# One encoder layer on one core: gating sum on VectorE inside the search rounds, and half-wide transposes for the queries

## The chip, the cores and the metric

One Trainium2 chip, of which the kernel uses one core. The metric is the time on the device of one execution, in microseconds (us). The engines are named as the profile names them: PE (TensorE, its matmuls), PEld (TensorE's weight loads), DVE (VectorE), ACT (ScalarE), POOL (GpSimd) and SP (SyncE).

## The reference, cut to what matters

One layer runs over 1024 prompt rows (tiles 0 to 7 of 128 rows) and 32 sample rows with a cache of 1024 positions (tile 8). The normalised input is projected to q, k, v, the indexer's qi, ki and wi, and u and vs. Every query scores all keys with the indexer, keeps the best 256 and attends over them. Beside it runs a gating unit. Both are concatenated and go through an output projection, a residual sum and a feed-forward block.

```
def _sgu(u, vs, ln_g, ln_b, w_s, b_s):
    u = gelu(u); vs = gelu(vs)                     # 4 groups of 128 channels
    vn = layer_norm(vs) * ln_g + ln_b
    s = einsum('gij,bcjge->bcige', wm, vn) + b_s   # over chunks of 128 positions
    return u * s

logits = einsum('bthd,btkhd->bthk', q, kg) * (HEAD_DIM ** -0.5)
```

The part of the gating unit that the change moves is `u * (W_s vn + b_s)`. Of the attention it changes how q gets from rows to columns.

## The kernel before, in words

**Precision.** Nearly every matmul splits its operands into a high and a low float16 half and runs three of the four products; weights are scaled by WS = 64.

**Order of the work.** The seven projections are made one after the other, in the order qi, ki, vs, u, k, v, q (`CHUNKS`, L61), each over the nine tiles. One tile of one projection is a step. Each engine has an instruction stream of its own, written out by hand as a `step` function, and parts of a step lag one or two tiles behind. `lagged(part, c, t, rep, lag)` calls a part for the tile `lag` before. Engines wait for each other by semaphores that count up.

**A step on PE** (L994): in u first the spatial product of the gating unit (`spatial`, L928, 12 matmuls into PSUM bank 6 or 7), then the projection (`main`, L911, 24 matmuls of 512 columns into bank 2 or 3, which waits for the evacuation of the projection two before), then the transposes of the tile two before (`post`, L940, into bank 4 or 5).

**A step on ACT** (L1471): `dup_q` for q (of the tile two before), the evacuation `E` (L1292; L1311 for u, L1316 for q and k, L1301 for v) into e32, the first sign count of the search, the cast `H` (L1319, L1346) of the tile before into the buffers hl, in u the evacuation of the spatial product `sgu_evac` (L1362, L1367: four 128x128 operations that scale and add the bias b_s, into r32), `R` (L1388, L1405), which takes the transposes of the tile two before out of PSUM, and the second sign count with the sum L1468. In the first two steps of each projection it casts weight pieces too (L438).

**A step on POOL** (L800): `A` (L716) makes the rotary embedding in four operations (L742 to L747) out of e32 into r32; for u it multiplies r32 (the gating sum) with e32 (gelu of u), L727. `B` (L749, L774) then subtracts the cast of the tile before, which gives the low half.

**The search on DVE.** From u to the fourth step of q the threshold of the best 256 keys is searched bit by bit, in 31 rounds (`bit_round`, L1864). A round counts five score tiles on DVE (L1833) and two on ACT (L1464), then waits for ACT's counts (L1839, the judge) and flips the bits (L1845). ACT's first sign count of the next round waits for that. Round b belongs to step b of u, k, v, q. In some rounds DVE also splits a weight piece (L444). After the search DVE makes the masks of the first four tiles (L1903 to L1918) and waits for the first logits (`peak`, L1941).

**Queries.** q needs each head's 64 columns turned, and the result twice, in partitions 0 to 63 and 64 to 127, once for the high half (unit 0) and once for the low half (unit 1). `H` writes every head's high half twice side by side into one buffer hl (1024 columns), `B` writes the low half into the other one, and `dup_q` (L1360) copies it beside itself. PE then turns 128 columns at a time, 8 transposes a unit. So one tile of q takes both buffers, and the cast of a tile waits until the split of the tile before has read it, and the split until PE has turned the tile before. At the end of q the last tiles are flushed (`flush`, L403): the last cast, two conversions of the cache (L1450), the last copies and evacuations. PE's first logits, DVE's first peaks and POOL's clearing of the packed queries wait for the last of them.

The loops over the steps 2 to 7 are hardware loops with two steps in a round, except where `LOOP` (L409) and the callers unroll them.

## Time and profile before

| | |
|---|---|
| median of 3 runs | 1440.9 us (1438.02 to 1442.58) |
| the profiled execution | 1443.37 us |
| its span, first to last instruction | 1441.6 us |
| granted TensorE clock, mean | 0.951 |
| busy shares | PE 90%, PEld 64%, DVE 57%, ACT 50%, POOL 35% |

The profile shows one execution. Times in it count from the start of the span. A line of a timeline has the start, the duration (of a merged run of equal instructions from the first start to the last end), engine, line of the kernel, operation, output and inputs, count, and in brackets the idle time of the engine before it with what ended it. M is the one large SBUF tensor, PS the PSUM, small a tensor of small values. The projections qi to q run until 478 us, the attention until 662 us, the output projection until 778 us, the feed-forward block to the end. The stage u runs from about 236 to 299 us, k to 356 us, v to 404 us, q to 478 us.

### The profile page before, as it was taken

The page shows a single profiled execution, that of the slowest core. Times are in us where ns is not written, and L with a number is a line of the kernel's source. Part 1 is how long each engine was busy: PE and PEld are TensorE (multiplying, and loading weights), DVE is VectorE, ACT ScalarE, POOL GpSimd, SP SyncE. Part 2 cuts the span into 40 slices and gives each one's busy share as a digit, 9 for nine tenths or more (in the row PEclk, how much of TensorE's full clock was granted, in tenths as well). Part 3 has the DMA queues.
Part 4 walks back from the last instruction along what each step waited for, and adds up shares of the span by engine and source line. Part 5 has one row for each costly group of instructions (what it writes and reads, how often), then busy time and mean ns, then how long its engine had stood idle before and what let it go on. Part 6 is the DMA issues. An engine that isn't in the chain of part 4 may idle for free.

```text
span 1441.6 us, 29366 instructions
## 1 busy us (share of the span) xinstructions
PE 1293.2 (90%) x10636; PEld 928.2 (64%) x10636; DVE 816.8 (57%) x1495; ACT 717.5 (50%) x1408; POOL 498.9 (35%) x542
## 2 busy tenths in 40 slices
PE   6868887999996666798997999999999998999997
PEld 3443333544443445565555888888888887888886
DVE  5324675889988565896656555666565552212022
ACT  5455788888784844893434444444444441001011
POOL 5872436367258531443003333333333300000001
PEclk9988999999999579999998999999999999999999
DMA  6121001212100310114231222112222127211013
GB/s 240 45 64 33 15 3 44 59 37 83 66 18 0 88 37 17 45 31 140 88 107 39 60 58 58 47 42 56 58 58 58 29 91 205 65 60 38 0 31 91
DMA packets 81597, 86.70 MB, mean 60 GB/s; under 512 B 6768, under 2 KB 63120, under 8 KB 81520
## 3 DMA queue, kind: packets, MB, share of 16 engines
q1 hardware_dynamic: 76112, 75.07, 18.1%
q10 hardware_dynamic: 4992, 9.51, 1.8%
q0 software_dynamic: 416, 1.08, 0.2%
q8 instruction: 49, 0.80, 0.2%
q14 instruction: 28, 0.23, 0.0%
HBM read 72.34 MB, written 13.31 MB: 59 GB/s over the span
## 4 chain that ended last, share of the span: by engine, by line
PE 55%; DVE 5%; ACT 4%; issue 2%; POOL 1%; DMA 1%; SPq 1%; POOLq 0%; ACTq 0%; DVEq 0%
PE PS L1189 29%; PE PS L1246 15%; PE PS L1152 6%; DVE M L1952 1%; PE PS L1069 1%; PE PS L1046 1%; DVE M L1941 1%; PE PS L1099 1%; ACT M L1542 1%; DMA M<-in_w_down 1%; ACT M L1531 1%; SPq L653 1%; PE PS L1233 1%; PE PS L1166 0%; PE PS L1066 0%
## 5 line engine op out<-in xcount | busy, mean ns | idle before, releaser
L1189 PE MATMUL PS<-M 128*128 128x264 f16 x3696 | 420.8, 278 | 9.6 <-ACT M L1646 9.6
L1189 PEld LDWEIGHTS PS<-M 128*128 128x128 f16 x3696 | 363.2, 98 | 66.6 <-ACT M L1646 10.2
L923 PE MATMUL PS<-M 128*128 128x512 f16 (+1 forms) x1512 | 309.4, 366 | 0.5 <-DVE M L1754 0.4
L1246 PE MATMUL PS<-M 128*128 128x256 f16 x2112 | 233.2, 274 | 6.6 <-DVE M L2166 6.6
L923 PEld LDWEIGHTS PS<-M 128*128 128x128 f16 (+1 forms) x1512 | 139.8, 104 | 153.1 <-issue 13.9
L1246 PEld LDWEIGHTS PS<-M 128*128 (+1 forms) x2112 | 207.2, 98 | 32.2 <-issue 7.5
L1833 DVE TENSOR_SCALAR_CACHE_REDUCE M<-M,small 128x384 f16<-128x384 f32 (+5 forms) x162 | 132.9, 881 | 0.8
L872 POOL TENSOR_TENSOR M<-M 128x264 f32<-128x264 f32 x44 | 34.7, 789 | 283.4 <-ACT M L1646 283.4
L688 POOL TENSOR_TENSOR small<-small 128x1 f32<-128x1 f32 x18 | 3.4, 189 | 317.1 <-ACT M L1738 237.3
L2005 DVE SCALAR_TENSOR_TENSOR M<-M 128x2048 f16<-128x2048 f32 (+1 forms) x44 | 88.9, 2025 | 36.1 <-ACT M L1584 36.1
L2166 DVE SCALAR_TENSOR_TENSOR M<-PS,M 128x256 f32 (+1 forms) x32 | 13.6, 424 | 165.3 <-PE PS L1246 165.3
L1646 ACT ACTIVATE M<-PS 128x264 f32<-128x264 f32 x132 | 51.3, 388 | 100.8 <-PE PS L1189 88.2
L1152 PE MATMUL PS<-M 128*128 128x512 f16 x384 | 84.2, 379 | 0.0
L1669 ACT ACTIVATE M<-M 128x1024 f16<-128x1024 f32 (+1 forms) x24 | 22.7, 978 | 117.1 <-PE PS L1233 82.7
L1464 ACT ACTIVATE M<-M,small 128x1056 f16<-128x1056 f32 x62 | 72.8, 1174 | 11.2 <-DVE small L1845 10.4
L1584 ACT ACTIVATE M<-M 128x2048 f16<-128x2048 f32 (+1 forms) x44 | 74.2, 1688 | 0.0
L1656 ACT ACTIVATE M<-M 128x264 f32 (+1 forms) x88 | 37.2, 423 | 70.2 <-DVE M L2090 36.3
L1069 PE MATMUL PS<-ident,M 128*128 128x128 f32 x306 | 57.0, 298 | 16.8 <-DVE M L1952 10.4
L1952 DVE TENSOR_TENSOR M<-PS,M 128x512 f16<-128x512 f32 (+3 forms) x102 | 53.5, 549 | 28.1 <-ACT M L1542 27.4
L2082 DVE TENSOR_TENSOR M<-PS,M 128x264 f32<-128x264 f32 x44 | 18.9, 432 | 83.7 <-PE PS L1189 82.3
L1152 PEld LDWEIGHTS PS<-M 128*128 128x128 f16 x384 | 37.5, 98 | 43.5
L1046 PE MATMUL PS<-M 128*128 128x512 f16 (+3 forms) x240 | 56.5, 361 | 9.5 <-DVE small L1941 8.1
(178 smaller groups left out, 1947.8 us busy)
## 6 DMA issues: line engine op xcount, KB each, us to landing
M<-in_w_in SPq DMA_DIRECT2D x24, 512.0 KB, 3.7
M<-in_w_gate SPq DMA_DIRECT2D x22, 512.0 KB, 4.0
M<-in_w_up SPq DMA_DIRECT2D x22, 512.0 KB, 5.2
M<-in_w_down SPq DMA_DIRECT2D x20, 512.0 KB, 4.1
M<-in_x_prompt SPq DMA_DIRECT2D x16, 512.0 KB, 5.0
M<-in_w_out SPq DMA_DIRECT2D x8, 512.0 KB, 3.8
h_scratch<-M ACTq DMA_DIRECT2D x8, 512.0 KB, 5.1
M<-h_scratch SPq DMA_DIRECT2D x16, 256.0 KB, 7.7
```

The source lines that it names most:

```text
L923: last = pe.matmul(bank(b)[:, 0:w], xnT[:, ds(t, 1), k, s, :].squeeze(1), wt[wbuf(c)][:, k * w:(k + 1) * w], start=(k == 0 and i == 0), st ...
L1046: last = pe.matmul(PSf[:, l_bank(j) * 512 + c0:l_bank(j) * 512 + c0 + n], qT[:, t, s, hd, :], key[:, hd, c0:c0 + n], start=(s == 0 and hd ...
L1069: last = pe.transpose(bank(pt_bank(g))[:, i * P:(i + 1) * P], LP[j % 4][:, (b0 + i) * P:(b0 + i + 1) * P], ident[:])
L1152: last = pe.matmul(bank(2 * p + d), mixT[:, t, k, s, :], wt[d][:, k * 512:(k + 1) * 512], start=(k == 0 and i == 0), stop=(k == KT - 1 and ...
L1189: last = pe.matmul(o, wsp[x][:, zw, wb, k * P:(k + 1) * P], ablk[:, ab, za, k * HT + s * SC:k * HT + (s + 1) * SC], start=(name not in kep ...
L1246: last = pe.matmul(o[:, 0:256], cols[:, ds(m * SC + r * P, P)], wt[dc % 2][:, f, :], start=(f == 0 and i == 0), stop=(f == FT - 1 and i == 2))
L1464: act.activation(sign_out, scores[:, o:o + TOK], ACT.Sign, scale=-1.0, bias=kth[:, j:j + 1], accum_out=signs[:, i:i + 1]).then_inc(signs_s ...
L1584: act.activation(wsp[x][:, 0, 4 * half:7 if half else 4, :], tb if half else raw[x], ACT.Copy, scale=WS).then_inc(w2_hi, 1)
L1646: act.activation(buf[s], bank(BANKS[x][s]["a"])[:, 0:SC], ACT.Copy).then_inc(kept, 1)
L1833: dve.tensor_scalar(dump[x][:, 0:S], scores[:, o:o + S], kth[:, j:j + 1], None, ALU.is_ge, ALU.add, accum_out=cnt[:, j:j + 1]).then_inc(se ...
L1952: dve.tensor_tensor(r[:, 1, 0:x * P], bank(pt_bank(g))[:, 0:x * P], r[:, 0, 0:x * P], ALU.subtract).then_inc(pt_ready, 1)
L2005: dve.scalar_tensor_tensor(out=wsp[x][:, 1, b, :], in0=tb if half else raw[x], scalar=WS, in1=wsp[x][:, 0, b, :], op0=ALU.mult, op1=ALU.su ...
```

## The change

The spatial product stays in PSUM. In round t + 1 of the search, behind its five counts and before its judge, DVE makes for each of the four groups one operation `(PSUM + bias) * gelu(u)`, in place in e32 (`gate`). The bias is scaled by 64 once, on POOL, at the first step of vs, so the gated value is 64 times as large as before. The cast and the split of u read e32; ACT's evacuation of the spatial product and POOL's multiplication are gone. So that the attention's half of the concatenated input has the same scale, its normalisation multiplies by 64, and the output projection scales by 1/64 twice.

For q the cast writes 512 columns into the first half of a buffer hl, the split writes the low half into its second half, and the next tile takes the other buffer. `dup_q` is gone. PE turns each head's 64 columns twice, into partitions 0 to 63 and 64 to 127: 16 transposes a unit in place of 8. PE's loop over the tiles of q is unrolled.

The diff, cut to its core:

```diff
@@ n_rope
-            return before(c, lambda n: n not in ("vs", "v")) + t
+            return before(c, lambda n: n not in ("vs", "u", "v")) + t
@@ wait_e_free
                 if NAMES[u[0]] == "vs":
                     eng.wait_ge(vs_norm, u[1] + 1)
+                elif NAMES[u[0]] == "u":
+                    eng.wait_ge(sub_done, n_cast(*u) + 1)
                 else:
                     eng.wait_ge(r_ready, n_rope(*u) + 1)
@@ POOL: A
                 if name == "u":
-                    pool.wait_ge(spatial_evac, t + 1)
-                    pool.wait_ge(evac_done, n_step(c, t) + 1)
-                    pool.tensor_tensor(r32[p], r32[p], e32[p], ALU.mult).then_inc(r_ready, 1)
                     return
@@ POOL: B
-                r = r32[p]
+                r = e32[p] if name == "u" else r32[p]
...
                 elif name == "q":
-                    pool.wait_ge(post_done, n_unit(c, t))
-                    out = hl[1 - s].rearrange("p (h r d) -> p h r d", h=HEADS, r=2)[:, :, 0, :]
-                    h = hl[s].rearrange("p (h r d) -> p h r d", h=HEADS, r=2)[:, :, 0, :]
-                    x = heads(r)
+                    out, x, h = hl[rep % 2][:, 512:1024], r, hl[rep % 2][:, 0:512]
@@ POOL: step
                         if isinstance(t, int) and t == 0:
                             pool.wait_ge(ln_loaded, 48)
+                            pool.tensor_scalar(bs, bs, WS, None, ALU.mult).then_inc(bs_scaled, 1)
@@ PE: spatial
                 if not isinstance(t, int) or t >= 2:
-                    pe.wait_ge(spatial_evac, t - 1)
+                    pe.wait_ge(gated, t - 1)
@@ PE: post
-                    if x == 0 and name != "q":
+                    if x == 0:
                         pe.wait_ge(sub_done, n_cast(c, t) + 1)
-                    elif x == 0:
-                        pe.wait_ge(cast_done, n_cast(c, t) + 1)
-                    else:
-                        pe.wait_ge(dup_done, t + 1)
...
+                    elif name == "q":
+                        for h in range(HEADS):
+                            v = hl[rep % 2][:, x * 512 + h * HD:x * 512 + (h + 1) * HD]
+                            for r in range(2):
+                                last = pe.transpose(ps[r * HD:(r + 1) * HD, h, :], v, ident16[:])
@@ PE: loop over the tiles
-                steps(pe, c, step, *(LOOP[c] if c != 1 else (NT, NT)))
+                steps(pe, c, step, *(LOOP[c] if c not in (1, NC - 1) else (NT, NT)))
@@ ACT: H
-                r = r32[p]
+                r = e32[p] if name == "u" else r32[p]
...
-                act.wait_ge(r_ready, n_rope(c, t) + 1)
+                if name == "u":
+                    act.wait_ge(gated, t + 1)
+                else:
+                    act.wait_ge(r_ready, n_rope(c, t) + 1)
...
-                act.wait_ge(post_done, n_unit(c, t) - 1)
+                act.wait_ge(post_done, n_unit(c, t) - (2 if name == "q" and t_above(t, 1) else 0 if name == "q" else 1))
                 if name == "q":
-                    act.wait_ge(sub_done, n_cast(c, t))
-                if name == "u":
+                    out, x = hl[rep % 2][:, 0:512], r
+                elif name == "u":
                     out, x = hl[s][:, 0:512], r
...
-                    if name == "q":
-                        out, x = v, heads(r).unsqueeze(2).broadcast_to([P, HEADS, 2, HD])
-                    else:
-                        out, x = v[:, :, 0, :], heads(r)
+                    out, x = v[:, :, 0, :], heads(r)
@@ ACT: dup_q and sgu_evac, with their calls
-            def dup_q(c, t, rep):
...
-                act.wait_ge(sub_done, n_cast(c, t) + 1)
-                v = hl[1 - n_unit(c, rep) % 2].rearrange("p (h r d) -> p h r d", h=HEADS, r=2)
-                act.activation(v[:, :, 1, :], v[:, :, 0, :], ACT.Copy).then_inc(dup_done, 1)
...
-            def sgu_evac(c, t, rep):
-                p = par(c, rep)
-                act.wait_ge(spatial_done, t + 1)
-                wait_r_free(act, c, t, p)
-                for g in range(GROUPS):
-                    last = act.activation(r32[p][:, g * P:(g + 1) * P], bank(6 + rep % 2)[:, g * P:(g + 1) * P],
-                                          ACT.Identity, scale=1 / WS, bias=bs[:, g:g + 1])
-                last.then_inc(spatial_evac, 1)
...
-                    lagged(dup_q, c, t, rep, 2)
...
-                    if NAMES[c] == "u":
-                        sgu_evac(c, t, rep)
...
-                    flush(dup_q, c, 2)
@@ DVE: bit_round
+            def gate(c, t):
+
+                p = par(c, t)
+                dve.wait_ge(spatial_done, t + 1)
+                dve.wait_ge(evac_done, n_step(c, t) + 1)
+                if t == 0:
+                    dve.wait_ge(bs_scaled, 1)
+                for g in range(GROUPS):
+                    v = e32[p][:, g * P:(g + 1) * P]
+                    last = dve.scalar_tensor_tensor(out=v, in0=bank(6 + t % 2)[:, g * P:(g + 1) * P],
+                                                    scalar=bs[:, g:g + 1], in1=v, op0=ALU.add, op1=ALU.mult)
+                last.then_inc(gated, 1)
+
             def bit_round(b):
 
                 base = SEL_FIRST + (b - 1) * SEL_ROUND
                 for j in range(ON_DVE):
                     count(j, base + max(0, j - 1))
+                if b <= NT:
+                    gate(cC["u"], b - 1)
                 dve.wait_ge(act_counted, b)
@@ DVE: normalise
-                dve.tensor_tensor(heads(o32_of(i)[:, half * 256:half * 256 + 256], 4),
...
-                                  ALU.mult).then_inc(o_ready, 1)
+                dve.scalar_tensor_tensor(out=heads(o32_of(i)[:, half * 256:half * 256 + 256], 4),
+                                         in0=heads(bank(o_bank(j))[:, 0:256], 4), scalar=WS,
...
+                                         op0=ALU.mult, op1=ALU.mult).then_inc(o_ready, 1)
@@ DVE: out_h (both places)
-                dve.scalar_tensor_tensor(out=h32[p], in0=PSf[:, p * D:(p + 1) * D], scalar=1 / WS, in1=xr[p],
+                dve.scalar_tensor_tensor(out=h32[p], in0=PSf[:, p * D:(p + 1) * D], scalar=WS ** -2, in1=xr[p],
```

## Rows read from the trace of the kernel before

**Rows 1.** The page's strip, PE, in 40 slices of 36 us, busy tenths.
```profile
PE   6868887999996666798997999999999998999997
```

**Rows 2.** Windows: length, busy us (count) of PE, PEld, DVE, ACT, POOL; clock; DMA.
```profile
237.00:246.00 9.00, 4.39 (x21) 2.45 (x22) 3.06 (x7) 8.93 (x19) 6.14 (x5) 0.62 0.03 7
...
260.00:299.00 39.00, 38.77 (x263) 20.63 (x261) 29.60 (x74) 34.34 (x74) 14.32 (x12) 1.00 0.18 54
299.00:356.00 57.00, 52.59 (x291) 24.57 (x290) 52.88 (x115) 46.09 (x79) 46.54 (x45) 1.00 0.23 74
...
458.00:478.00 20.00, 4.60 (x49) 3.50 (x46) 7.60 (x6) 11.04 (x15) 12.19 (x11) 0.64 0.09 27
```

**Rows 3.** Timeline of ACT, second step of q.
```profile
412.24 1.18 ACT L1464 ACTIVATE M<-M,small 128x1056 f16<-128x1056 f32 x1 [2.08 <-DVE small L1845]
```

**Rows 4.** Timeline of PE, start of u.
```profile
241.61 1.48 PE L935 MATMUL PS<-M 128*128 x12 [5.19 <-ACT M L1367]
...
251.93 0.92 PE L956 MATMUL PS<-ident,M 128*128 128x128 f16 x8 [2.53 <-POOL M L774]
...
261.00 5.34 PE L923 MATMUL PS<-M 128*128 128x512 f16 x24
```

**Rows 5.** Timeline of ACT, start of u.
```profile
236.49 0.57 ACT L1311 ACTIVATE M<-PS 128x512 f32<-128x512 f32 x1
...
240.34 1.10 ACT L1367 ACTIVATE M<-PS,small 128x128 f32<-128x128 f32 x4
...
246.79 0.62 ACT L1346 ACTIVATE M<-M 128x512 f16<-128x512 f32 x1
```

**Rows 6.** Timeline of POOL, start of u.
```profile
249.42 1.26 POOL L727 TENSOR_TENSOR M<-M 128x512 f32<-128x512 f32 x1 [1.30 <-ACT M L1367]
250.65 1.15 POOL L774 TENSOR_TENSOR M<-M 128x512 f16<-128x512 f32 x1
```

**Rows 7.** Timeline of DVE, start of u: the judge of rounds 1 and 2.
```profile
242.87 0.28 DVE L1839 TENSOR_SCALAR small<-small 128x7 uint32<-128x7 f32 x1 [12.49 <-ACT small L1468]
...
250.77 1.06 DVE L1839 TENSOR_SCALAR small<-small 128x7 uint32<-128x7 f32 x1 [2.28 <-ACT small L1468]
```

**Rows 8.** Groups by line and shape, 404 to 478 us: busy us, mean ns | idle before.
```profile
L742 POOL TENSOR_TENSOR M<-M 128x512 f32<-128x512 f32 x9 | 12.6, 1396 | 16.1 <-ACT M L1316 16.1
...
L1360 ACT ACTIVATE M<-M 128x512 f16<-128x512 f16 x9 | 5.6, 626 | 16.4 <-POOL M L774 16.3
```

**Rows 9.** Timelines of POOL, then of ACT, in the last steps of q.
```profile
449.90 1.40 POOL L774 TENSOR_TENSOR M<-M 128x512 f16<-128x512 f32 x1
...
466.86 1.15 POOL L774 TENSOR_TENSOR M<-M 128x512 f16<-128x512 f32 x1
471.97 1.15 POOL L774 TENSOR_TENSOR M<-M 128x512 f16<-128x512 f32 x1 [3.97 <-PE PS L960]
...
451.34 0.63 ACT L1360 ACTIVATE M<-M 128x512 f16<-128x512 f16 x1 [3.82 <-POOL M L774]
...
468.12 1.06 ACT L1346 ACTIVATE M<-M 128x1024 f16<-128x1024 f32 x1 [5.08 <-POOL M L774]
...
473.16 0.63 ACT L1360 ACTIVATE M<-M 128x512 f16<-128x512 f16 x1 [2.42 <-POOL M L774]
...
475.89 1.94 ACT L1405 ACTIVATE M<-PS 128x1024 f16<-128x1024 f16 x2 [0.28 <-PE PS L960]
```

**Rows 10.** Groups by line and shape, the whole span.
```profile
L1246 PE MATMUL PS<-M 128*128 128x256 f16 x2112 | 233.2, 274 | 6.6 <-DVE M L2166 6.6
...
L1952 DVE TENSOR_TENSOR M<-PS,M 128x128 f16<-128x128 f32 x18 | 5.1, 283 | 3.7 <-ACT M L1542 3.7
```

**Rows 11.** The chain that ended last, last stage: start, us, what.
```profile
1252.37 2.07 PE PS L1233 x66
1254.44 57.75 PE PS L1246 x528
```

**Rows 12.** Timeline of DVE, its first peak.
```profile
478.45 0.29 DVE L1941 CUSTOM_DVE_ANT_0 M<-PS,cmask 128x128 f32<-128x128 f32 x1 [12.67 <-PE PS L1046]
```

More of the change, by code:

```diff
@@ L259, in encoder_step @@
         rope_mul, r_ready = sem("rope_mul"), sem("r_ready")
-        cast_done, sub_done, dup_done = sem("cast_done"), sem("sub_done"), sem("dup_done")
+        cast_done, sub_done = sem("cast_done"), sem("sub_done")
         post_done, post_evac = sem("post_done"), sem("post_evac")
@@ L264, in encoder_step @@
                                                  ("vs_mean", "vs_sq", "vs_rstd", "vs_norm", "vs_tmp", "vs_g"))
-        v_sub = sem("v_sub")
-        spatial_done, spatial_evac = sem("spatial_done"), sem("spatial_evac")
+        v_sub, bs_scaled = sem("v_sub"), sem("bs_scaled")
+        spatial_done, gated = sem("spatial_done"), sem("gated")
         score_mm, score_relu, score_acc = sem("score_mm"), sem("score_relu"), sem("score_acc")
@@ L380, in t_below, with t_above @@
             return not isinstance(t, int) or t < bound
+        def t_above(t, bound):
+            return not isinstance(t, int) or t > bound
         def lagged(part, c, t, rep, lag):
@@ L1352, in next_pieces @@
                         piece_hi(act, i)
-            def dup_q(c, t, rep):
-                if NAMES[c] != "q":
-                    return
-                act.wait_ge(sub_done, n_cast(c, t) + 1)
-                v = hl[1 - n_unit(c, rep) % 2].rearrange("p (h r d) -> p h r d", h=HEADS, r=2)
-                act.activation(v[:, :, 1, :], v[:, :, 0, :], ACT.Copy).then_inc(dup_done, 1)
-            def sgu_evac(c, t, rep):
-                p = par(c, rep)
-                act.wait_ge(spatial_done, t + 1)
-                wait_r_free(act, c, t, p)
-                for g in range(GROUPS):
-                    last = act.activation(r32[p][:, g * P:(g + 1) * P], bank(6 + rep % 2)[:, g * P:(g + 1) * P],
-                                          ACT.Identity, scale=1 / WS, bias=bs[:, g:g + 1])
-                last.then_inc(spatial_evac, 1)
             def vs_squares(c, t, rep):
@@ L1963, in normalise @@
                     dve.wait_ge(o_lo, i - (ATT_TILES[i - 1] == LAST))
-                dve.tensor_tensor(heads(o32_of(i)[:, half * 256:half * 256 + 256], 4),
-                                  heads(bank(o_bank(j))[:, 0:256], 4),
-                                  rinv[i % 2][:, half * 4:half * 4 + 4].unsqueeze(2).broadcast_to([P, 4, HD]),
-                                  ALU.mult).then_inc(o_ready, 1)
+                dve.scalar_tensor_tensor(out=heads(o32_of(i)[:, half * 256:half * 256 + 256], 4),
+                                         in0=heads(bank(o_bank(j))[:, 0:256], 4), scalar=WS,
+                                         in1=rinv[i % 2][:, half * 4:half * 4 + 4].unsqueeze(2).broadcast_to([P, 4, HD]),
+                                         op0=ALU.mult, op1=ALU.mult).then_inc(o_ready, 1)
             for i in range(EARLY_MASKS):
@@ L2019, in out_h @@
                         dve.scalar_tensor_tensor(out=h32[p][0:DEC], in0=PSf[j * DEC:(j + 1) * DEC, p * D:(p + 1) * D],
-                                                 scalar=1 / WS, in1=h32[p][0:DEC] if j else xr[p][0:DEC], op0=ALU.mult,
+                                                 scalar=WS ** -2, in1=h32[p][0:DEC] if j else xr[p][0:DEC], op0=ALU.mult,
                                                  op1=ALU.add).then_inc(h_part if j < 3 else h_ready, 1)
                     return
-                dve.scalar_tensor_tensor(out=h32[p], in0=PSf[:, p * D:(p + 1) * D], scalar=1 / WS, in1=xr[p],
+                dve.scalar_tensor_tensor(out=h32[p], in0=PSf[:, p * D:(p + 1) * D], scalar=WS ** -2, in1=xr[p],
                                          op0=ALU.mult, op1=ALU.add).then_inc(h_ready, 1)
```

## The prediction

> **What bounds the kernel now.** I read the page's strip of busy shares first: PE is at nine tenths nearly everywhere behind the attention [rows 1], so nothing that this change touches there can matter. The change works in the projections u and q, 237 to 478 us. The stage windows [rows 2] are read next, and each stage has another limit. From 260 to 299 us (steps 4 to 9 of u) PE is busy 38.77 of 39.00 us. From 299 to 356 us (k) DVE is busy 52.88 of 57 us: the search rounds pace the work, and where k, v and the first steps of q meet the search, ACT waits for its next candidate (2.08 us in [rows 3]). At two places no engine is full. From 237 to 246 us PE is busy 4.39 of 9 us, and from 458 to 478 us 4.60 of 20. There chains of waits set the time, and the timelines of single engines show them: [rows 4 to 7] for the start of u, [rows 8, 9] for q. The chain that ended last agrees for q: from 453 to 478 us it goes through POOL's rotary operations, the split, the copy of the low half, and the evacuations.
>
> The sum is made against the profiled execution, 1443.4 us (its span is 1441.6 us), which is 2.5 us above the median of the runs, 1440.9 us.
>
> **Part A, the start of u.** PE's third spatial product waits 5.19 us, until 241.61 [rows 4], for ACT's first eviction of a gating sum at 240.34, which ACT reaches only behind a sign count and a normalisation [rows 5]. DVE meanwhile stands idle: its judge waits 12.49 us for ACT's count [rows 7]. With the change the gate is DVE's. It needs the spatial product (long done) and the evacuation of u, which ends at 236.49 + 0.57 = 237.06. No row has this operation; the nearest is a 128x128 operation of two tensors from PSUM, 283 ns [rows 10]. Four are 1.13 us (below, 0.8 us, if they overlap as the search counts do; above, see the rivals). So the first gate ends at 238.2, and the third spatial product starts 3.3 us earlier.
>
> PE's next wait is for the first transposes, until 251.93 [rows 4]. They follow POOL's split at 250.65, which follows POOL's multiplication at 249.42, which waited for ACT's second eviction [rows 6]. With the change the eviction is gone from ACT (1.0 us of its time, so the cast of 246.79 [rows 5] comes at 245.8) and the multiplication from POOL. The cast ends at 246.4; POOL first splits the last vs tile, until about 247.05, then the u tile, 1.15 us, until 248.2. The transposes start at 248.3, 3.6 us earlier. The second gate is done at about 248.6, in time for the next spatial product, and the fourth projection starts 3.6 us earlier too. At the change from u to k ACT is behind, not PE, and one more eviction of 1.0 us is gone. **Part A: 4.5 us**, between 2.5 (late gate) and 6. Above 4.5: the granted clock was 0.62 in 237 to 246 us [rows 2], so a PE that idles less may run at 2.4 GHz sooner; I take nothing for that.
>
> **The gates of the other steps.** PE's step is 39 us / 6 = 6.5 us. DVE is idle 39.00 - 29.60 = 9.4 us of these six, 1.57 us a step [rows 2], more than 1.13. Its idle time stands before the judge, which waits for ACT's count, and the gate stands just there. So it is costed at nothing. In the four rounds that also split a weight piece the slack is smaller, some 0.3 us a round is overrun, and PE's double-buffered bank (a projection waits for the evacuation two before it) covers that. Without this cover it is 9 x 1.13 = 10.2 us. Behind the gate on DVE stand the judge and the flip of the bits, for which ACT's first sign count waits, and behind that count ACT's casts; the gate itself waits for nothing later than ACT's evacuation of the same step. POOL loses nine multiplications of 1.26 us, hidden except in the chain above.
>
> A rule against it: two engines can block each other. DVE's judge took 1.06 us at 250.77 [rows 7] while POOL's split ran from 250.65 to 251.80 [rows 6]. The Trainium skill (SBUF — State Buffer, "SBUF: two separate sides") says that VectorE and GpSimd share one pair of SBUF ports, held for a whole instruction, by a VectorE operation in a two-port mode or with two SBUF inputs. By it the judge should block, as the row shows, and the gate, with one tensor in PSUM, should not; no run shows the gate. If it did block, once a step behind the split, 1.15 us a step would come on top, which leads into the second rival below.
>
> **Part B, what is carried.** k and v keep their instructions. All engines enter k 4.5 us earlier, and DVE's rounds then run as before. Nothing is added or lost.
>
> **Part C, the steps of q.** Today ACT runs, in each step: the copy of the low half of the tile two before, then the evacuation. The copy waits for POOL's split, 16.4 us in nine steps, and POOL's first rotary operation waits for the evacuation, 16.1 us in nine [rows 8]. That is a ring: evacuation, four rotary operations, split of the tile before, copy, next evacuation. At 449.90 POOL starts the split, the copy starts at 451.34 as it ends, and only then comes the evacuation [rows 9]. With the change the copy is gone (626 ns x 9), the cast writes 512 instead of 1024 columns (about 0.62 instead of 1.05 us), and the evacuation waits for PE alone. What comes next is PE and POOL themselves. PE needs a projection, about 5.2 us (5.34 with the fill, [rows 4]), and 32 transposes instead of 16; POOL needs 5.2 to 6.4 us a step.
>
> The transposes are the open price. The tile is the loaded operand and the identity streams 128 columns, so 32 half-wide ones cost twice PE's time unless two run side by side. In the last stage 528 full-wide multiplications of 256 columns take 57.75 us, 109 ns each, and 66 with only 32 loaded columns 2.07 us, 31 ns each [rows 11]: narrow ones with different output partitions do run beside each other. The change alternates between output partitions 0 to 63 and 64 to 127, so I take pairs: 32 x 31 ns = 1.0 us a tile, against 16 x 55 ns = 0.9 us now (half of 109 ns, for 128 columns); the other end is 32 x 55 = 1.8 us.
>
> The Trainium skill (TensorEngine Tiling (Array Packing), "Key Properties") lets tiles load and multiply in parallel, but says that a change of the tiling mode drains the engine. By that each tile of q would pay two drains; were each as long as one multiplication from start to end (274 ns, [rows 10]), 18 of them would add 4.9 us and give 1432.4 us. The trace bears out no such drain: the 66 narrow ones end at 1254.44, just when the full-wide ones start [rows 11]. It is counted as one way into the second rival.
>
> So PE's step is about 6.2 us and POOL's 5.2 to 6.4 us. Half of POOL's 16.1 us falls into the steps behind the search, and I take away about half a step's wait in six steps: **4.6 us**, between 0.5 (transposes one by one) and 6.
>
> **Part D, the end of q.** From the last tile's rotary end (466.86) to the last evacuation (475.89 + 1.94 = 477.83) it is 11.0 us [rows 9]. The last cast waits for the split of the tile before (468.12), the last split for PE's transposes of that tile (471.97, 3.97 us idle), then come the copy (473.16), the transposes and two evacuations. With two buffers that each hold a whole tile, the last cast runs beside the split of the tile before. What is left: that split 1.15 us, one unit of transposes 1.0 us, four evacuations of 0.97 us in a row, and 0.3 us of waits, 6.3 us. **Part D: 4.6 us**, between 0.7 (transposes one by one at the low clock) and 5. PE's, DVE's and POOL's attention work waits for this end. DVE had been idle 12.67 us before its first peak [rows 12]; that is the ceiling of parts C and D together, and then the early masks are late next.
>
> **Small things.** The bias is scaled once on POOL under the vs stage; 18 normalisations get a second scalar (no row here; the plain ones and the three-operand ones from PSUM differ by about 10 ns, 0.2 us in all); the scale in the output projection is another constant. PE's q loop is unrolled: the queue fetches more code, hidden behind 24 matmuls a step, at most 1 us. Together 0.3 us.
>
> **Sum.** 4.5 + 4.6 + 4.6 - 0.3 = 13.4 us. 1443.4 - 13.4 = 1430.0 us for an execution like the profiled one, and 1440.9 - 13.4 = 1427.5 us for the median.
>
> **Rivals.**
> 1. *One by one* (0.15): the half-wide transposes don't pair. PE's step is 5.2 + 1.8 + a wait, about the 7.2 us of today, and the tail gets four units at double price. Parts C and D shrink to 0.5 + 0.7: 1440.9 - 5.6 = 1435.3 us. For it: no row has 64 loaded columns. Against: the rows with 32.
> 2. *One part does not arrive* (0.19): the gates block behind POOL and DVE carries u's gain away, or POOL's operations stretch under DVE's mask steps so that q's steps stay. That takes 4.5 us off: 1432.0 us. For it: POOL's first rotary operation averages 1396 ns in q [rows 8] because of such stretches.
> 3. *Slower* (0.05): every one of the four gate operations waits as the judge did, 1.06 us [rows 7]. A gate is then 4.24 us, the nine cost 9 x (4.24 - 1.57) = 24.0 us, less the 13.4: 1451.5 us. It decides from 1.57 + 13.4 / 9 = 3.1 us a gate. Against: POOL has one split of 1.15 us in a step of u after the change.
> 4. *Absorbed* (0.06): the attention does not start earlier, because masks or the cache's conversions on POOL (now less far ahead) end last. The time stays within 0.3%, about 4.3 us, which is what a measurement of this kernel can tell from no change: 1439 us.
>
> **Numbers.** The forecast has 0.55. Faster by over 0.3%: the forecast, rival 2 and most of rival 1 (0.12), 0.86. Within: rival 4 and the rest of rival 1, 0.09. Slower: 0.05. The range goes from 1423.5 (part A and the whole 12.67 us) to 1436.5 us (one by one, with a late gate).
>
> **What would show it.** Right: the wait of the third spatial product falls from 5.19 to about 2 us; DVE's gate is about 1.1 us in four, and its waits for ACT's count shrink by that; PE stays full from about 256 to 295 us; the steps of q are 6.2 to 6.5 us; 32 transposes take about 1 us; 6 us lie between the last rotary operation and the last evacuation; everything behind is shifted as it is. Wrong: 32 transposes in 1.8 us or more; gates over 2 us; DVE without idle time in u and PE waiting for the gate; a first peak that waits for masks.

## The result, and the profile after

| | before | after |
|---|---|---|
| median of 6 runs each | 1440.91 us (1438.02 to 1442.58) | 1427.88 us (1424.59 to 1430.13) |
| ratio after to before, 95% interval | | 0.9909 (0.9890 to 0.9928) |
| profiled execution, its span | 1443.37 us, 1441.6 us | 1430.13 us, 1428.3 us |
| granted clock, mean | 0.951 | 0.961 |

The change makes the kernel 13.0 us faster. Lines have moved: `main` is L924, `spatial` L936, the transposes L953 (q: L959), the gate L1854, the judge L1820, ACT's cast L1348, its evacuations L1313, L1318 and L1390, the rotary operations L745 to L750, the masks L1899 to L1914, the peaks L1937. Behind the attention nothing looks different: the page's strip of PE, which answers to [rows 1]:

```profile
PE   6877888999997677899997999999999998999997
```

The windows of the changed kernel [rows 2], same columns; the stages lie 5 us earlier in k and v and 12 us earlier behind q:

```profile
237.00:246.00 9.00, 6.48 (x36) 3.11 (x36) 5.16 (x13) 8.93 (x18) 4.98 (x5) 1.00 0.03 7
...
256.00:294.00 38.00, 38.00 (x261) 20.59 (x260) 36.51 (x102) 28.43 (x50) 6.94 (x6) 1.00 0.20 56
294.00:351.00 57.00, 53.23 (x297) 24.96 (x295) 52.86 (x113) 46.10 (x79) 46.57 (x45) 1.00 0.23 74
...
451.00:466.00 15.00, 4.97 (x100) 4.33 (x100) 8.01 (x6) 8.71 (x12) 12.70 (x11) 0.77 0.13 34
```

From 256 to 294 us PE has no idle time left and DVE is busy 36.51 of 38 us: the gates fill what was idle there. k (294 to 351 us) is what it was. From 237 to 246 us ACT is busy 8.93 of 9 us, as it was before the change [rows 2]: it is the full engine there, and the gate no longer has to wait its turn in ACT's stream. At the end of q POOL is the fullest engine, 12.70 of 15 us.

The start of u. The timeline of PE, which answers to [rows 4]:

```profile
238.49 1.19 PE L936 MATMUL PS<-M 128*128 x12 [2.04 <-DVE M L1854]
...
248.39 0.83 PE L953 MATMUL PS<-ident,M 128*128 128x128 f16 x8 [3.43 <-POOL M L774]
...
250.29 6.22 PE L924 MATMUL PS<-M 128*128 128x512 f16 x24
```

DVE and then POOL in the same stretch ([rows 6, 7]):

```profile
237.19 1.12 DVE L1854 SCALAR_TENSOR_TENSOR M<-PS,small,M 128x128 f32<-128x128 f32 x4 [6.79 <-issue]
241.89 1.30 DVE L1820 TENSOR_SCALAR small<-small 128x7 uint32<-128x7 f32 x1 [3.57 <-ACT small L1453]
...
247.50 1.12 DVE L1854 SCALAR_TENSOR_TENSOR M<-PS,small,M 128x128 f32<-128x128 f32 x4
...
253.06 1.12 DVE L1854 SCALAR_TENSOR_TENSOR M<-PS,small,M 128x128 f32<-128x128 f32 x4
...
237.00 1.26 POOL L797 TENSOR_TENSOR M<-M 128x512 f32<-128x512 f32 x1
...
241.90 1.27 POOL L797 TENSOR_TENSOR M<-M 128x512 f32<-128x512 f32 x1
245.99 2.27 POOL L774 TENSOR_TENSOR M<-M 128x512 f16<-128x512 f32 x2 [2.82 <-ACT M L1329]
```

The third spatial product waits 2.04 us instead of 5.19, and its releaser is now the gate. Four gate operations take 1.12 us beside POOL's operations (237.19 beside the one of 237.00, 247.50 beside the subtractions from 245.99 to 248.26), and the same 1.12 us where POOL is idle (253.06; POOL's next operation starts at 258.97). The judge beside POOL's operation of 241.90 took 1.30 us.

In q, the groups by line and shape from 399 to 466 us [rows 8]:

```profile
L745 POOL TENSOR_TENSOR M<-M 128x512 f32<-128x512 f32 x9 | 12.7, 1410 | 11.9 <-ACT M L1318 11.5 <-POOL M L774 0.3
...
L959 PE MATMUL PS<-ident,M 128*64 128x128 f16 x288 | 11.1, 238 | 13.6 <-POOL M L774 13.3 <-ACT M L1390 0.4
```

The copy and its 16.4 us of waits are gone; POOL's wait ahead of its first rotary operation fell from 16.1 to 11.9 us. Timelines of PE, POOL, ACT and DVE in q and at its end ([rows 9, 12]):

```profile
411.12 5.35 PE L924 MATMUL PS<-M 128*128 128x512 f16 x24
416.40 1.08 PE L959 MATMUL PS<-ident,M 128*64 128x128 f16 x32
417.42 5.35 PE L924 MATMUL PS<-M 128*128 128x512 f16 x24
...
438.09 5.35 PE L924 MATMUL PS<-M 128*128 128x512 f16 x24
...
445.30 5.35 PE L924 MATMUL PS<-M 128*128 128x512 f16 x24
451.81 1.08 PE L959 MATMUL PS<-ident,M 128*64 128x128 f16 x32 [1.16 <-POOL M L774]
460.25 1.92 PE L959 MATMUL PS<-ident,M 128*64 128x128 f16 x32 [7.35 <-POOL M L774]
462.52 1.62 PE L959 MATMUL PS<-ident,M 128*64 128x128 f16 x32 [0.35 <-ACT M L1390]
...
437.69 1.47 POOL L745 TENSOR_TENSOR M<-M 128x512 f32<-128x512 f32 x1 [0.67 <-ACT M L1318]
...
444.48 2.16 POOL L745 TENSOR_TENSOR M<-M 128x512 f32<-128x512 f32 x1 [0.25 <-POOL M L774]
...
451.89 1.42 POOL L745 TENSOR_TENSOR M<-M 128x512 f32<-128x512 f32 x1
453.27 2.16 POOL L746 TENSOR_TENSOR M<-M 128x256 f32<-128x256 f32 x1
...
456.91 1.86 POOL L750 TENSOR_TENSOR M<-M 128x512 f32<-128x512 f32 x1
458.73 2.58 POOL L774 TENSOR_TENSOR M<-M 128x512 f16<-128x512 f32 x2
...
461.35 1.94 ACT L1390 ACTIVATE M<-PS 128x1024 f16<-128x1024 f16 x2 [0.88 <-PE PS L959]
463.62 1.94 ACT L1390 ACTIVATE M<-PS 128x1024 f16<-128x1024 f16 x2 [0.33 <-PE PS L959]
...
452.40 2.52 DVE L1906 TENSOR_TENSOR_SCAN M<-M 128x768 f16<-128x768 f16 x1
...
466.08 0.29 DVE L1937 CUSTOM_DVE_ANT_0 M<-PS,cmask 128x128 f32<-128x128 f32 x1 [6.90 <-PE PS L1048]
```

32 half-wide transposes take 1.08 us. PE's step without a wait is 6.30 us (411.12 to 417.42), but in the last steps PE waits for POOL's split, and POOL's operations of the last tile are long: 2.16 us where the same shape took 0.72 us early in q. What answers to [rows 3, 10, 11] is as it was: ACT waits 2.09 us for the flip of the bits in the second step of q, a full-wide multiplication of the last stage takes 274 ns, and 66 narrow ones take 2.07 us. The last evacuation ends at 465.56 (before: 477.83).

Where the time went is read best from one point to the next inside an execution, because the profiled executions differ by up to 5 us ahead of u, where the kernels are the same but for the scaling of the bias on POOL. The table counts from the moment at which PE falls idle ahead of the third spatial product of u (236.42 us in the profile of before, 236.45 in that of after).

| kernel | PE's wait there | k's first rotary operation | end of q's last rotary operation | last evacuation of q | first peak |
|---|---|---|---|---|---|
| before | 5.19 | 64.11 | 230.48 | 241.41 | 242.03 |
| after | 2.04 | 58.81 | 222.32 | 229.11 | 229.63 |
| gate alone | 2.07 | 58.86 | 224.28 | 235.22 | 235.84 |
| queries alone | 5.24 | 64.22 | 228.42 | 235.21 | 235.73 |
| one half at a time | 2.07 | 58.88 | 222.85 | 230.48 | 231.10 |
| late gate | 6.75 | 61.34 | 225.22 | 232.01 | 232.53 |
| one tile | 2.04 | 58.82 | 222.31 | 231.58 | 232.20 |
| masks late | 2.06 | 58.84 | 217.47 | 223.95 | 244.72 |
| fourth mask waits | 2.06 | 58.86 | 219.46 | 225.94 | 228.12 |

So 5.3 us came from u, 2.9 us from the steps of q (8.16 less 5.30 at its last rotary operation), 4.1 us from the end of q: 12.3 us at the last evacuation. From the first peak to the end of the span it is 963.15 us before and 962.2 us after.

### The profile page after: what moved, and what is told of

It reads as the page before. It is cut to its first block, busy times and chain, and to the rows that moved or that the text cites. A ratio compares the mean times of both kernels' runs of the same rounds, so it can differ in the third digit from the quotient of the medians.

```text
span 1428.3 us, 29477 instructions
## 1 busy us (share of the span) xinstructions
PE 1286.5 (90%) x10780; PEld 925.6 (65%) x10780; DVE 825.6 (58%) x1531; ACT 700.0 (49%) x1363; POOL 491.1 (34%) x534
## 3 DMA queue, kind: packets, MB, share of 16 engines
q0 software_dynamic: 416, 1.08, 0.2%
## 4 chain that ended last, share of the span: by engine, by line
PE 65%; DVE 9%; issue 8%; ACT 8%; POOL 7%; DMA 2%; SPq 1%; POOLq 0%; ACTq 0%; DVEq 0%
PE PS L1191 29%; PE PS L1248 15%; PE PS L924 8%; PE PS L1154 6%; DVE M L1814 3%; DVE M L1948 1%; PE PS L1071 1%; POOL M L774 1%; PE PS L1048 1%; PE PS L1101 1%; DVE M L1937 1%; ACT M L1449 1%; ACT M L1523 1%; DMA M<-in_w_down 1%; POOL M L746 1%
## 5 line engine op out<-in xcount | busy, mean ns | idle before, releaser
L924 PE MATMUL PS<-M 128*128 128x512 f16 (+1 forms) x1512 | 306.1, 363 | 0.5 <-DVE M L1735 0.4
L924 PEld LDWEIGHTS PS<-M 128*128 128x128 f16 (+1 forms) x1512 | 137.9, 102 | 151.6 <-issue 10.3
L774 POOL TENSOR_TENSOR M<-M 128x512 f16<-128x512 f32 (+2 forms) x54 | 57.5, 1065 | 40.1 <-ACT M L1348 35.9
```

The lines of the kernel that those rows point to most:

```text
L774: pool.tensor_tensor(out, x, h, ALU.subtract).then_inc(sub_done, 1)
L924: last = pe.matmul(bank(b)[:, 0:w], xnT[:, ds(t, 1), k, s, :].squeeze(1), wt[wbuf(c)][:, k * w:(k + 1) * w], start=(k == 0 and i == 0), st ...
```

## The experiments

**The two parts alone.** Theory: the gains of u and of q add up, since k and v carry the first through.

```diff
 gate alone: q keeps dup_q, the 1024-column cast and the 128-column transposes
 queries alone: ACT keeps sgu_evac, POOL the product r32 * e32, DVE makes no gate
```

> Only the gate's part of the change; the queries are cast, copied and turned as in the kernel before. If the start of u is what this part gives (in the two profiles the first rotary operation of k starts at 300.53 us before and at 295.26 us after, 5.3 us earlier) and everything behind is only shifted: k starts at about 295.3 us, q's steps and its end are as before (11.0 us from the last rotary operation to the last evacuation), and the time is 1440.9 - 5.3 = 1435.6 us, within 2 us. Rival, the gate's 9 x 1.1 us on DVE are paid later by the search: 1440 us or more. Rival, the whole gain comes from here: 1428 us.

Measured: 1434.65 us, ratio 0.9958 (0.9944 to 0.9972).

> Only the queries' part of the change; the gating sum is evacuated by ACT and multiplied on POOL as before. If the parts add up (in the profiles the last evacuation of q moved by 12.3 us, 5.3 of them before k): the stages up to v are as before, the last evacuation of q comes about 7.0 us earlier, at 470.8 us, and the time is 1440.9 - 7.0 = 1433.9 us, within 2 us. Rival, the two parts need each other: both alone give less, in sum under 9 us. Rival, POOL's own work in q sets the steps and nothing but the end gains: 4 us, 1437 us.

Measured: 1433.62 us, ratio 0.9949 (0.9932 to 0.9965). The product of the two ratios is 0.9907, the change has 0.9909. The table says the same: 6.2 us earlier at the last evacuation by either part (241.41 less 235.22 and less 235.21), 12.3 us by both. The gate alone brings 5.25 us up to k and 0.95 us more in q, where the expectation had the steps as before; no run shows why. The queries alone bring nothing up to k, 2.1 us in the steps and 4.1 us at the end.

**Transposes, one half at a time.** The price left open was whether half-wide transposes run side by side.

```diff
-                        for h in range(HEADS):
-                            v = hl[rep % 2][:, x * 512 + h * HD:x * 512 + (h + 1) * HD]
-                            for r in range(2):
+                        for r in range(2):
+                            for h in range(HEADS):
+                                v = hl[rep % 2][:, x * 512 + h * HD:x * 512 + (h + 1) * HD]
```

> The changed kernel with the same 32 transposes of a tile in another order: per unit first the eight into partitions 0 to 63, then the eight into 64 to 127. If half-wide transposes run two at a time only when neighbours go to different output partitions: 32 take about 1.8 us in place of 1.08, PE's step in q grows from 6.3 to 7.1 us and the end of q by 2 to 3 us; the time is about 1434 us (1432 to 1437). Rival, narrow ones are cheap in any order: 1.08 us a tile and 1428 us.

Measured: 1429.49 us, ratio 0.9926 (0.9909 to 0.9943). The timeline of PE in this kernel, a tile inside q and the last one:

```profile
416.32 1.39 PE L959 MATMUL PS<-ident,M 128*64 128x128 f16 x32
...
462.99 2.33 PE L959 MATMUL PS<-ident,M 128*64 128x128 f16 x32 [0.34 <-ACT M L1390]
```

Eight transposes into the same half in a row make 32 take 1.39 us instead of 1.08, and 2.33 instead of 1.62 us for the last tile. So the order matters, and alternating is the better one. Neither the expectation (1.8 us, 1434 us) nor its rival (1.08 us) came true: even in this order 32 are faster than the 1.8 us put down for one by one. The last evacuation comes 1.4 us later, the medians are 1.6 us apart; the two intervals overlap, so the time alone doesn't show it, the rows do. What truly serial half-wide transposes cost was not measured.

**The gate behind the wait for ACT's counts.** The gate can be worth its place only if DVE reaches it before that wait.

```diff
-                if b <= NT:
-                    gate(cC["u"], b - 1)
                 dve.wait_ge(act_counted, b)
+                if b <= NT:
+                    gate(cC["u"], b - 1)
```

> The changed kernel with DVE's gate behind its wait for ACT's counts in place of before it. If the gate is free only because it stands in that wait, and the first round is what matters: the first gate starts at about 241.9 instead of 237.2 us, the third spatial product waits about 6.6 instead of 2.0 us, later rounds (where DVE no longer waited) are the same, and the time is about 4.5 us longer, 1432.4 us. Rival, every round pays: 9 x 1.1 us, 1438 us. Rival, the place does not matter: 1428 us.

Measured: 1431.92 us, ratio 0.9938 (0.9921 to 0.9956). The timelines of DVE and of PE in this kernel, start of u:

```profile
241.89 1.13 DVE L1854 SCALAR_TENSOR_TENSOR M<-PS,small,M 128x128 f32<-128x128 f32 x4 [11.49 <-ACT small L1453]
242.93 0.25 DVE L1820 TENSOR_SCALAR small<-small 128x7 uint32<-128x7 f32 x1
...
243.18 1.48 PE L936 MATMUL PS<-M 128*128 x12 [6.75 <-DVE M L1854]
244.45 7.46 PE L924 MATMUL PS<-M 128*128 128x512 f16 x24
```

The gate starts 4.7 us later (241.89 against 237.19), and PE waits 6.75 us, more than before the change. k's first rotary operation comes 2.5 us later than in the changed kernel, the last evacuation of q 2.9 us, and the median is 4.0 us longer; the intervals of the two ratios just overlap, so the 2.5 and 2.9 us of the traces are the safer size. The order of two calls on DVE is worth about half of what the gate brings (2.5 of 5.3 us up to k).

**One tile in flight.** Is part D due to the two buffers that now hold a whole tile each?

```diff
-                act.wait_ge(post_done, n_unit(c, t) - (2 if name == "q" and t_above(t, 1) else 0 if name == "q" else 1))
+                act.wait_ge(post_done, n_unit(c, t) - (0 if name == "q" else 1))
```

> The cast of a tile of q waits until PE has turned the tile before, so that only one tile is between the cast and the transposes at a time, although two buffers are there. Theory (part D comes from two tiles in flight): in the steps the cast comes behind the transposes of the tile before anyway, within some 0.5 us a step, but at the end the last cast (458.80 in the changed kernel) has to wait for the transposes of the tile before, which end at 462.2, and then come cast 0.6, split 1.2, transposes and evacuations. From the last rotary operation to the last evacuation it becomes 9 to 9.5 us instead of 6.8, and the time about 1430.5 us, 2 to 3 us above the changed kernel. Rival (the end of q is bound by POOL's splits and ACT's evacuations, whichever buffers there are): 1428 us.

Measured: 1431.45 us, ratio 0.9929 (0.9912 to 0.9945). The timelines of ACT and of PE at the end of q:

```profile
461.88 0.63 ACT L1348 ACTIVATE M<-M 128x512 f16<-128x512 f32 x1 [6.81 <-PE PS L959]
...
464.60 1.92 PE L959 MATMUL PS<-ident,M 128*64 128x128 f16 x32 [2.83 <-ACT M L1390]
```

The last cast waits for PE, and the tail from the last rotary operation to the last evacuation is 9.27 us instead of 6.79. The steps of q don't change at all (222.31 in the table). So 2.5 of the 4.1 us of part D come from the second tile in flight. The other 1.6 us stay when only one tile is in flight; that they come from the copy that is gone and the cast of half the width is argued, no run separates them.

**All early masks behind q.** Part C had come out too small (2.9 instead of 4.6 us). Theory: POOL's operations stretch beside DVE's masks.

```diff
+            dve.wait_ge(post_evac, n_unit(NC - 1, LAST) + 2)
             for i in range(EARLY_MASKS):
                 for k in range(7):
                     mask_step(i, k)
-            dve.wait_ge(post_evac, n_unit(NC - 1, LAST) + 2)
```

> DVE makes its four early masks behind the end of q instead of beside q. Theory (part C was too large because POOL's operations stretch under DVE's mask steps): POOL's five operations of a tile fall back to 1.27 + 0.73 + 0.73 + 1.27 + 1.16, about 5.2 us, in the last tiles; the steps of q become PE's, about 6.3 to 6.6 us; the last rotary operation ends some 3 us earlier than 458.8, and the last evacuation too. The whole time is longer all the same, by about the 31 us of masks that now stand ahead of the first peaks, less the 3 us. Rival (the steps of q are bound by PE or by ACT, not by POOL): the last evacuation stays at 465 to 466 us.

Measured, one run: 1446.12 us. The timelines of POOL, last tile of q, and of DVE:

```profile
448.88 1.27 POOL L745 TENSOR_TENSOR M<-M 128x512 f32<-128x512 f32 x1 [1.13 <-ACT M L1318]
450.10 0.72 POOL L746 TENSOR_TENSOR M<-M 128x256 f32<-128x256 f32 x1
...
451.58 1.26 POOL L750 TENSOR_TENSOR M<-M 128x512 f32<-128x512 f32 x1
...
475.71 1.76 DVE L1906 TENSOR_TENSOR_SCAN M<-M 128x768 f16<-128x768 f16 x1
...
479.61 0.56 DVE L1914 TENSOR_SCALAR M<-M 128x768 f32<-128x768 f32 x1
```

POOL's four rotary operations of the last tile take 4.0 us (448.88 to 452.84) instead of 6.9 (451.89 to 458.77). The last rotary operation ends 4.85 us earlier than in the changed kernel, and POOL waits for ACT again. ACT's evacuations of the last projections follow each other every 6.2 to 6.4 us, PE's own step, instead of 6.4 to 7.2 us. The stretching is mutual: the scan of 768 columns takes 1.76 us here, and 2.52 us beside POOL in the changed kernel; the four masks take 20.7 us (459.43 to 480.17) instead of 30.4 (428.78 to 459.18). Only because they now stand ahead of the first peak is the whole slower. The expectation's 31 us for them was the stretched size.

**Only the fourth mask waits.** If both sides pay, the mask that meets POOL's last tile should wait until that tile is through; DVE was idle 6.90 us ahead of its first peak anyway.

```diff
             for i in range(EARLY_MASKS):
+                if i == EARLY_MASKS - 1:
+                    dve.wait_ge(r_ready, n_rope(NC - 1, LAST) + 1)
```

> Only the fourth early mask waits, for POOL's last rotary operation of q. Theory (as in the run with all masks late): POOL's operations of the last tile are unstretched, the last rotary operation ends 2 to 3 us earlier (at about 456), the last evacuation at about 463; DVE ends the fourth mask at about 465.5, and the first peak comes about as before or 1 us earlier: 1426.5 to 1428 us. Rival (the steps of q are not bound by POOL): the last evacuation stays, the mask comes late, and the time grows by 1 to 4 us, 1429 to 1432 us.

Measured: 1422.94 us, ratio 0.9879 (0.9860 to 0.9897), better than expected. The timelines of POOL and DVE:

```profile
449.04 0.72 POOL L746 TENSOR_TENSOR M<-M 128x256 f32<-128x256 f32 x1
...
450.52 1.26 POOL L750 TENSOR_TENSOR M<-M 128x512 f32<-128x512 f32 x1
...
451.81 1.01 DVE L1899 TENSOR_SCALAR_CACHE_REDUCE M<-M,small 128x768 f16<-128x768 f32 x1 [6.37 <-POOL M L750]
...
460.44 0.27 DVE L1937 CUSTOM_DVE_ANT_0 M<-PS,cmask 128x128 f32<-128x128 f32 x1
```

The last rotary operation ends 2.9 us earlier and the last evacuation 3.2 us; the first peak follows the mask without idle time, 1.5 us earlier. It comes 2.2 us behind the last evacuation (228.12 less 225.94), where it came 0.5 us behind it, so the mask is now late by some 1.7 us.

**The same wait in the kernel before, and repeats.** The edit is the one above, in the kernel before; the other runs are the changed kernel itself and the waiting mask once more.

> The kernel before, with the one edit of the last run: its fourth early mask waits for POOL's last rotary operation of q. Theory (the two halves of the gain are separate: the stretching of POOL's last tile was there before the change, and in the run with the changed kernel the wait brought some 4.5 us): POOL's four rotary operations of the last tile fall from 6.5 to 4.1 us, the last evacuation comes 2.5 us earlier, and the attention gives back less; 1435.5 to 1438.5 us, ratio 0.9965 to 0.9985. Rival (the wait helps only where the copy of the low half is gone, since without it the end of q waits for splits and copies): 1440 us or more.

Measured: 1439.81 us, ratio 0.9991 (0.9976 to 1.0007). The timelines of POOL and DVE:

```profile
457.31 0.72 POOL L743 TENSOR_TENSOR M<-M 128x256 f32<-128x256 f32 x1
...
472.19 0.29 DVE L1941 CUSTOM_DVE_ANT_0 M<-PS,cmask 128x128 f32<-128x128 f32 x1 [4.91 <-PE PS L1046]
```

POOL is unstretched here too, and counted as in the table the first peak comes 2.0 us earlier (240.00). The median missed the expected 1435.5 to 1438.5 us. A gain of 2.0 us is inside the interval of the ratio, which tells it neither from the expected gain nor from none, so whether the wait shortens the kernel before is not shown.

> The changed kernel as it is, beside the run with the mask in the kernel before, to have its time of the same chip and hour: 1426 to 1429.5 us, ratio 0.990 to 0.9925 to the kernel before. The run with the waiting fourth mask then stands at 0.996 to 0.998 of it.

Measured: 1427.22 us, ratio 0.9893 (0.9872 to 0.9914).

> The changed kernel with the waiting fourth mask, a second time, now on the same chip as the changed kernel itself. Theory: the first peak comes 1.5 us earlier by the first trace, so the time is 1.5 us (up to 4.5, as the first medians said) below that of the changed kernel beside it. Rival: the first difference was chance, and the two agree within 1 us.

Measured: 1422.96 us, ratio 0.9875 (0.9852 to 0.9898).

> The changed kernel beside it: 1426 to 1429.5 us, ratio 0.989 to 0.9925.

Measured: 1427.47 us, ratio 0.9893 (0.9873 to 0.9913). The timeline of PE in this execution of the changed kernel, start of u:

```profile
238.44 1.48 PE L936 MATMUL PS<-M 128*128 x12 [2.04 <-DVE M L1854]
239.72 6.43 PE L924 MATMUL PS<-M 128*128 128x512 f16 x24
248.35 0.71 PE L953 MATMUL PS<-ident,M 128*128 128x128 f16 x8 [2.20 <-POOL M L774]
```

So the waiting mask is twice some 4.5 us below the changed kernel in the median, and it is the best version found. Over all runs of the two the lowest times differ by 2.8 us (1421.08 and 1423.84), the highest by 3.2 us (1426.95 and 1430.13). The traces account for 1.5 to 2 us: from k's first rotary operation to the first peak it is 169.3 us in the first execution with the wait, 169.4 in the second, and 170.8 to 171.3 in the three of the changed kernel. The first peak of the second execution comes 2.5 us earlier, but 1.0 us of that was won ahead of k, which the wait doesn't touch: its fourth projection of u took 5.35 us instead of 6.22, at a granted clock of 1.00 from 246 to 256 us instead of 0.83. The rest stays open: in the two profiled executions with the wait the stretch ahead of u, where the kernels are the same, was 4.1 and 2.0 us shorter, at a higher granted clock (1.00 against 0.96 from 140 to 180 us), and from the first peak to the end they took 960.4 and 959.7 us where the changed kernel took 961.1 to 962.2. With the gate alone the stretch ahead of u was shorter by 5.1 us in its profiled execution as well, and there the median came out as the parts say.

## Why the prediction was right, point by point

The sum was 13.4 us; the medians differ by 13.0 us, the profiled spans by 13.3. Its terms were off in both directions, and part of the agreement is that they cancel.

- **Part A, 4.5 us predicted, 5.3 measured.** The chain ran as written: third spatial product 3.1 us earlier (238.49; 3.3 predicted), transposes 3.5 us (248.39; 3.6), fourth projection 3.64 us (250.29; 3.6). The end was undersized: 0.6 us more were won in PE's steps and 1.04 us at ACT's first evacuation of k, where 0.9 us had been put down for both. In the profiled execution the clock was rightly counted at nothing, though it did rise: granted 1.00 from 237 to 246 us instead of 0.62, and the third projection took 5.35 instead of 6.52 us, but PE then waited 3.43 us for POOL's split where it had waited 2.53. The last run shows it in the same kernel: at a granted clock of 0.81 its third projection took 6.43 us, PE waited 2.20 us, and the transposes started 11.95 us behind the table's mark, against 11.94. Where the clock was high in the fourth projection too, in the second execution with the waiting mask, k came 1.0 us earlier, so up to that much was open above the term. With the late gate the clock was low (0.58), PE waited for nothing behind the projection, and its 7.46 us counted in full. Two readings were wrong without harm. "At two places no engine is full" does not hold from 237 to 246 us: ACT was busy 8.93 of the 9 us, which is why a gating sum that waited for ACT came late. The window from 260 to 299 us holds the last five steps of u and the first of k, not steps 4 to 9 of u.
- **The gates of the other steps, nothing predicted.** Right: PE had no idle time from 256 to 294 us, and the nine gates took 10.1 us in DVE's idle time; it left 0.25 us a step (38.00 less 36.51 over six). The rival in which each gate operation waits as the judge did would have shown four in 4.24 us; they took 1.12. The Trainium skill (SBUF — State Buffer, "SBUF: two separate sides") has only a VectorE operation in a two-port mode or with two SBUF inputs exclude GpSimd, so not one with one of its two tensors in PSUM, and the gates agree: 1.12 us beside POOL (247.50) and without it (253.06).
- **Part B, nothing predicted.** Right: the first evacuation of q comes 5.3 us earlier, as k's first rotary operation did.
- **Part C, 4.6 us predicted, 2.9 measured.** The step that failed is "POOL needs 5.2 to 6.4 us a step". It is 5.2 us only where DVE's masks don't run: from one tile's first rotary operation to the next it was 6.8 and 7.4 us in the last steps (437.69, 444.48, 451.89), and in the last tile the four rotary operations alone took 6.9 us. So PE's last steps were 6.9 and 7.2 us long (projections at 431.21, 438.09 and 445.30), not the 6.2 to 6.5 us that were named as a sign of being right. The stretching had been seen in the rows and put into the second rival as a chance, not into the term. Without it the steps of q would have given 7.7 us (2.9 and the 4.85 of the late masks). By the same section of the Trainium skill a VectorE operation with two SBUF inputs and a GpSimd operation exclude each other; the rows agree that both lose: 0.72 to 2.16 us on POOL, 1.76 to 2.52 us on DVE.
- **The transposes.** The price was right: 1.08 us for 32 (1.0 predicted), so the first rival falls. That they run in pairs, the reason given for it, is shown only in part: they take 34 ns each when the halves alternate and 43 ns in groups of eight of one half, and both are below the 55 ns that were put down for one by one. Neither is there a drain of the size that was weighed, two of 274 ns a tile: the projection starts 1.02 us behind the first transpose (416.40 to 417.42), 32 times 32 ns, and the transposes start 5.28 us behind the projection, 0.1 us more than the full-wide ones of u behind theirs (5.18). The Trainium skill (TensorEngine Tiling (Array Packing), "Key Properties") states a drain at each change of the mode; no run here shows one longer than that 0.1 us.
- **Part D, 4.6 us predicted, 4.1 measured.** The tail is 6.79 us instead of 6.3. Most of the difference is the split ahead of it, which takes 1.5 us beside the last mask (458.73 until the transposes start at 460.25), not 1.15. The first unit of transposes took 1.1 us (460.25 until ACT's evacuation starts at 461.35; 1.0 predicted), and the evacuations with the wait between them 4.2 us (461.35 to 465.56), as predicted. That the second buffer carries 2.5 us of the gain, the run with one tile in flight shows.
- **Absorbed.** That rival falls too: DVE was idle 6.90 us ahead of its first peak, so no mask was late; it is what was left of the 12.67 us of before [rows 12], and what the waiting fourth mask then used. From the first peak to the end the profiled executions of all kernels took 960 to 965 us, so that the 1 us by which the changed kernel's was shorter there can't be told from that spread; neither can the 0.3 us of the small things.
- **Sums.** By the prediction's own terms the first rival is 5.4 us and 1435.5 us, not 5.6 and 1435.3, and the range goes from about 1424 to 1437.5 us, not from 1423.5 to 1436.5. The measured 1427.9 us is inside either way.

## What to carry to other kernels

An engine's idle time ahead of a wait is the place for moved work, as long as that work itself waits for nothing so late; behind the same wait, half its worth was lost. A buffer that holds a whole tile of both halves lets the last tile's steps overlap at a stage's end, where there is no other work to hide them. When two engines stretch each other's operations, a wait that keeps the off-path engine out of the critical tile can be a gain for both (in the changed kernel it was, in the kernel before the time does not show it); price such a stage with the stretched durations, from the rows in which the two run together.

## What the runs showed of the hardware that was not expected

- The order of half-wide transposes changes their rate: 32 that alternate between the halves of the output partitions took 1.08 us, in groups of eight of the same half 1.39 us.
- VectorE's mask steps and GpSimd's rotary operations cost each other a third to a half of their time: 30.4 against 20.7 us for four masks, 6.9 against 4.0 us for four rotary operations. Even a VectorE operation of 128x7 elements took 1.30 us beside a GpSimd operation (0.22 us alone), while 128x128 operations with an input in PSUM were not held up.
- The granted clock behind PE's wait for the third spatial product does not follow the length of that wait alone. Taken over the same 9 us, 0.55 to 9.55 us behind the table's mark, it was on average 0.58 where PE waited 6.75 us, and 0.62, 0.62 and 0.81 in the three executions in which it waited 5.19 to 5.24 us. Where it waited 2.04 to 2.08 us, it was 1.00 in four executions and 0.81 in five; of the changed kernel itself 1.00 in two and 0.81 in one.
